# Differential attention: q's factor on the scores, roots and reciprocals over 192 columns, k rotated raw

## The reference, cut to what matters

```python
def rms_norm(x, g):
    x32 = x.astype(F32)
    y = x32 * lax.rsqrt(jnp.mean(x32 * x32, axis=-1, keepdims=True) + EPS)
    return (y * g.astype(F32)).astype(x.dtype)
...
def diff_softmax_pair(q, k, v, lam, scale):
    s = jnp.einsum('bqnd,bknd->bnqk', q, k).astype(F32) * scale
    p = jax.nn.softmax(s, axis=-1)
    ...
    w = p[:, :, 0] - lam * p[:, :, 1]
    return jnp.einsum('bhqk,bkhe->bqhe', w.astype(v.dtype), v)
...
    q = rms_norm(q.reshape(bsz, n, 2 * DIFF_HEADS, DIFF_DH), qn_g)
    k = rms_norm(k.reshape(bsz, n, 2 * DIFF_HEADS, DIFF_DH), kn_g)
    ...
    q_l = apply_axial_rope(q_l, cos, sin)      # x * cos + rot(x) * sin
    k_l = apply_axial_rope(k_l, cos, sin)
    ...
    o = rms_norm(o, subln_g) * (1.0 - lam_init)
    return (o.reshape(bsz, n, D_INNER) * jax.nn.silu(z)) @ w_out
```

## Time and profile before

| | us |
|---|---|
| median of three runs | 4011.03 (3999.76 to 4014.48) |
| the profiled execution | 4011.99 |
| its span, first to last instruction | 4010.3 |
| TensorE busy with matmuls | 3700.1, 92% |
| VectorE busy | 2045.9, 51% |
| ScalarE busy | 1197.8, 30% |
| the differential stage | from 1683 to 2852 |
| granted TensorE clock, mean of the span | 0.976 of full speed |

### The profile page before, as it was taken

How to read it: one execution, slowest core, us unless ns; L and a number is a source line. 1 busy time by engine, 2 the same in 40 slices (tenths; PEclk the granted TensorE clock), 3 DMA queues, 4 the chain that set the end, 5 groups by cost and what they waited for, 6 DMA issues and landing times.

```text
span 4010.3 us, 44586 instructions
## 1 busy us (share of the span) xinstructions
PE 3700.1 (92%) x16234; PEld 2354.2 (59%) x16234; DVE 2045.9 (51%) x3693; ACT 1197.8 (30%) x2200; POOL 143.2 (4%) x227
## 2 busy tenths in 40 slices
PE   5998999998889999899999999998798999999989
PEld 2445488873446888665656565564454555555554
DVE  3744353644545545455666666666214555555541
ACT  1213210112332101133434434343102454545530
POOL 6600000000000000000000000000000000000000
PEclk8998999999999999999999999999899999999999
DMA  7521334340013342410111011100011122212211
GB/s 149 143 75 48 95 95 106 89 112 24 21 53 105 95 116 74 116 37 27 32 31 31 26 31 31 31 26 26 23 51 58 53 58 58 58 53 57 58 32 53
DMA packets 456433, 246.27 MB, mean 61 GB/s; under 512 B 44256, under 2 KB 448352, under 8 KB 456320
## 3 DMA queue, kind: packets, MB, share of 16 engines
q1 hardware_dynamic: 420384, 216.15, 19.6%
q0 software_dynamic: 14144, 28.36, 2.7%
q10 hardware_dynamic: 21792, 0.22, 0.4%
HBM read 229.83 MB, written 14.80 MB: 61 GB/s over the span
## 4 chain that ended last, share of the span: by engine, by line
PE 79%; DVE 12%; ACT 4%; issue 2%; ACTq 1%; DMA 0%; DVEq 0%; SPq 0%
PE bank L466 19%; PE bank L1188 15%; PE bank L328 10%; PE bank L1709 8%; DVE rs L1934 4%; PE bank L1695 3%; PE bank L1036 3%; PE bank L1100 3%; PE bank L863 2%; PE bank L1731 2%; PE bank L1081 2%; PE bank L1742 2%; PE bank L846 1%; PE bank L1677 1%; PE bank L1345 1%
## 5 line engine op out<-in xcount | busy, mean ns | idle before, releaser
L1188 PE MATMUL bank<-hT,ring 128*128 128x512 f32 (+1 forms) x1664 | 634.1, 531 | 11.3 <-ACT hT L1599 6.0
L1709 PE MATMUL bank<-hT,ring 128*128 128x512 f32 x1504 | 509.0, 490 | 20.0 <-DVE big L1961 16.3
L1188 PEld LDWEIGHTS bank<-hT,ring 128*128 128x128 f32 x1664 | 311.1, 191 | 289.0 <-issue 276.2
L1709 PEld LDWEIGHTS bank<-hT,ring 128*128 128x128 f32 x1504 | 280.6, 190 | 244.4 <-issue 207.1
L328 PE MATMUL bank<-big,ring 128*128 128x512 f32 (+1 forms) x1024 | 389.2, 543 | 12.3 <-DVE big L1973 8.4
L328 PEld LDWEIGHTS bank<-big,ring 128*128 128x128 f32 x1024 | 195.8, 192 | 204.2 <-issue 183.9
L1088 ACT ACTIVATE arena<-bank 128x512 f32<-128x512 f32 (+2 forms) x224 | 118.4, 528 | 462.3 <-PE bank L1081 462.0
L466 PE MATMUL bank<-big,arena 128*128 128x256 f32 x1024 | 228.8, 379 | 0.0
L466 PEld LDWEIGHTS bank<-big,arena 128*128 128x128 f32 x1024 | 194.6, 190 | 26.5
L1056 DVE CUSTOM_DVE_ANT_0 arena<-bank,big 128x512 f32<-128x512 f32 (+2 forms) x152 | 101.3, 666 | 201.4 <-PE bank L1036 201.4
L1695 PEld LDWEIGHTS bank<-ring,hT 128*128 128x128 f32 x1536 | 179.2, 193 | 30.4 <-DVE arena L1928 17.1
(11 more groups left out here) (293 smaller groups left out, 5276.0 us busy)
## 6 DMA issues: line engine op xcount, KB each, us to landing
ring<-in_mlp_w SPq DMA_DIRECT2D x128, 512.0 KB, 5.5
ring<-in_a_w_in SPq DMA_DIRECT2D x64, 512.0 KB, 4.0
ring<-in_b_w_in SPq DMA_DIRECT2D x64, 512.0 KB, 4.0
ring<-in_mod_w SPq DMA_DIRECT2D x48, 512.0 KB, 4.0
ring<-in_even_w_in SPq DMA_DIRECT2D x32, 512.0 KB, 4.0
bias_d<-tb POOLq DMA_DIRECT2D x96, 128.0 KB, 3.3
big<-bias_d POOLq DMA_DIRECT2D x16, 768.0 KB, 5.4
ring<-in_a_w_out SPq DMA_DIRECT2D x16, 512.0 KB, 3.7
```

What stands on the lines that cost most here:

```text
L1188: mm = pe.matmul(bk(b + n)[0:m, 0:z - a], ring[s][:, k, 0:m], (rhs or hcol)(k, a, z), start=k == 0, stop=k == kt - 1)
L1709: mm = pe.matmul(flatb[2][:, a:z], ring[s][:, k, :], hT[:, k, a:z], start=k == 0, stop=k == KT - 1)
```

## The change

q's factor is no longer multiplied into q. The raw q (kept in the tile rs, called d_q) is rotated with a matrix that has the gain in it (rotq); its sum of squares is taken with the tokens on the partitions (six matmuls with two output columns), 12 columns per head in d_rq, and the factor is applied as the scale of the exponentials (exps) and in the negated maxima. k is rotated raw with its gain (rotk), and its factor multiplied in at the end (normed_k). For k and for the output the sum of squares goes to four groups of 32 partitions, 192 columns each, so that root and reciprocal run over 128 x 192 (d_rn, in the tile tb); a new matmul (broadcast, with the selecting matrices sel) spreads the factor over all partitions and 768 columns of bank 3, from which normed_k and y_normed read it. The places of the steps in each engine's order change with it.

```diff
+            dve.wait_ge(md_c, 8)
+            dve.tensor_scalar(rotq, rotx, cols[:, 5:6], None, ALU.mult).then_inc(md_c, 1)
+        def dve_rotk(dve):
+            dve.tensor_scalar(rotk, rotx, cols[:, 6:7], None, ALU.mult).then_inc(md_c, 1)
...
-        STEP = ["Tc'", "T0", "sq", "T1", "rq", "sk", "T2", "rk", "so'", "T3"]
+        STEP = ["Tc'", "T0", "rq", "sq", "T1", "rk", "sk", "T2", "bk", "so'", "bo'", "T3"]
...
 pe_dif:
                 if t == 0:
-                    pe.wait_ge(ds["m2"], h * 2 + 2)
+                    pe.wait_ge(ds["nr"], h + 1)
...
-                for a, z in spans(TT):
-                    mm = pe.matmul(flatb[3][:, a:z], lhs, d_sq[:, a:z], start=True, stop=True)
+                for j in range(4):
+                    mm = pe.matmul(flatb[3][32 * j:32 * j + 32, 0:G], lhs, d_sq[:, G * j:G * j + G],
+                                   start=True, stop=True, skip_group_check=True)
...
+            def stats_q():
+                pe.wait_ge(ds["sq"], st.sq["q"])
+                st.n_free(pe, "sq")
+                for t in range(6):
+                    mm = pe.matmul(flatb[3][:, 2 * t:2 * t + 2], d_sq[:, P * t:P * t + P], per_head,
+                                   start=True, stop=True, skip_group_check=True)
+            def broadcast(x, n):
+                pe.wait_ge(ds["rr"], n)
+                st.n_free(pe, x)
+                for i in range(2):
+                    for half_, r in enumerate((LO, HI)):
+                        mm = pe.matmul(bank[3][:, half_, G * i:G * i + G], sel[i][r, :], d_rn[r, :],
+                                       start=True, stop=True, skip_group_check=True)
...
             if make:
+                rotate_q()
                 project(1, "k", 0, 4)
-                stats("sq", st.sq["q"], b64)
+                stats_q()
...
             if make:
+                rotate_k()
                 project(2, "v", 0, 2)
-                rotate("rq", g * 2 + 1)
-                project(2, "v", 2, 4)
-                stats("sk", st.sq["k"], b64)
-                project(2, "v", 4, 6)
+                stats("sk", st.sq["k"], b64[:, 48:80])
+                project(2, "v", 2, 6)
...
             if make:
+                broadcast("bk", st.rr["k"])
                 project(3, "z", 0, 2)
-                rotate("rk", g * 2 + 2)
+            if old:
+                stats("so'", st.sq["o'"], ones[:, 0:32])
+            if make:
                 project(3, "z", 2, 4)
             if old:
-                stats("so'", st.sq["o'"], ones)
+                broadcast("bo'", st.rr["o'"])
...
 act_dif:
-                        mm = act.activation(d_p[s], flatb[s][:, 0:TT], ACT.Exp, bias=dst[:, 4 + s:5 + s],
-                                            accum_out=dst[:, 8 + s:9 + s])
+                        c = 2 * t + s
+                        mm = act.activation(d_p[s], flatb[s][:, 0:TT], ACT.Exp, scale=d_rq[e][:, c:c + 1],
+                                            bias=dst[:, 4 + s:5 + s], accum_out=dst[:, 8 + s:9 + s])
...
-                act.activation(rs[:, :], flatb[3][:, 0:TT], ACT.Sqrt, scale=1.0 / w, bias=eps).then_inc(ds["nf"], 1)
+                act.activation(d_rn, flatb[3][:, 0:G], ACT.Sqrt, scale=1.0 / w, bias=eps).then_inc(ds["nf"], 1)
...
 dve_dif:
+            def inverse(x, n):
+                st.n_done(dve, x)
+                dve.reciprocal(d_rn, d_rn).then_inc(ds["rr"], 1)
+            def normed_k():
+                dve.wait_ge(ds["bc"], st.rr["k"])
+                dve.wait_ge(ds["m2"], g * 2 + 2)
+                dve.tensor_tensor(spread(dk_(ge)), spread(d_nrm), bank[3][:, :, 0:2 * G], ALU.mult)\
+                    .then_inc(ds["nr"], 1)
...
             def y_normed(h, x, use):
-                st.n_done(dve, use)
-                dve.reciprocal(rs[:, :], rs[:, :]).then_inc(ds["rr"], 1)
-                dve.wait_ge(ds["rr"], st.sq[x])
+                dve.wait_ge(ds["bc"], st.rr[x])
...
             if on:
                 maxima(1)
+            if make:
+                rotated_q()
+            if on:
                 probs(1)
             if make:
-                normed("q", 0, 5)
-                evac(1, 1)
+                evac(1, d_raw)
+                inverse_q()
             if on:
                 maxima(2)
+            if make:
+                rotated_k()
+            if on:
                 probs(2)
             if make:
-                rotated(0, [(dq_(ge), ALL)])
-                normed("k", 1, 6)
+                inverse("sk", "k")
             if on:
                 maxima(3)
+            if make:
+                normed_k()
+            if on:
                 probs(3)
-            if make:
-                rotated(1, [(dk_(ge), ALL)])
             if old:
                 gated(h - 1, 1 - e, "o'", "pv'")
+                inverse("so'", "o'")
+                y_normed(h - 1, "o'", "so'")
             if on:
                 maxima(4)
                 probs(4)
-            if old:
-                y_normed(h - 1, "o'", "so'")
...
 before the stage, on TensorE and on VectorE:
+            pe.wait_ge(ds["ax"], 32)
+            pe.wait_ge(md_c, 12)
             run_dif(pe_dif, pe)
...
             dve_modulated(dve, 0, 0)
-            dve.wait_ge(ds["ax"], 16)
+            dve_rotk(dve)
+            dve.wait_ge(ds["ax"], 32)
             run_dif(dve_dif, dve)
```

More of the change, by code:

```diff
@@ L87, in constants @@
     c[:, C_AX + 512:C_AX + 1024] = np.tile(np.sin(ang), (2, 1))
+    for p in range(P):
+        if p % 16 == 0:
+            o = C_SEL + 128 * (p // 32 % 2) + 64 * (p // 16 % 2)
+            c[p, o:o + 64] = 1.0
     return c
@@ L1618, in program, with spread @@
         d_raw, d_nrm, d_sq = part(7680, TT), part(8448, TT), part(9216, TT)
+        d_q = rs[:, :]
+        G = TT // 4
+        tbf = tb[:, :, :].rearrange("p a b -> p (a b)")
+        d_rn = tbf[:, 0:G]
+        d_rq = [tbf[:, G + 12 * e:G + 12 * e + 12] for e in range(2)]
+        sel = [cst[:, C_CZ + P * i:C_CZ + P * i + P] for i in range(2)]
+        rotq, rotk = cst[:, C_RP:C_RP + P], cst[:, C_RM:C_RM + P]
+        per_head = b64.rearrange("p (s n) -> p s n", s=2)[:, :, 0]
+        def spread(x):
+            return x.rearrange("p (a n) -> p a n", a=2)
         axc = [part(9984, 512), part(10496, 512)]
@@ L1852, in act_dif @@
             if make:
-                act.wait_ge(ds["nr"], g * 2 + 1)
+                if old:
+                    act.wait_ge(ds["y"], h)
                 root(st.sq["k"], 64)
@@ new lines, in rotated_k @@
+            def rotated_k():
+                dve.wait_ge(ds["rot"], g * 2 + 2)
+                dve.tensor_tensor(d_t2, bank[3][:, 0, :], axc[1], ALU.mult).then_inc(ds["nf"], 1)
+                dve.tensor_scalar(d_nrm[:, S:TT], d_raw[:, S:TT], cols[:, 6:7], None, ALU.mult)
+                dve.scalar_tensor_tensor(out=d_nrm[:, 0:S], in0=d_raw[:, 0:S], scalar=cols[:, 6:7], in1=axc[0],
+                                         op0=ALU.mult, op1=ALU.mult).then_inc(ds["m1"], 1)
+                dve.wait_ge(ds["m1"], g * 2 + 2)
+                st.n_done(dve, "rk")
+                dve.tensor_tensor(d_nrm[:, 0:S], d_nrm[:, 0:S], d_t2, ALU.add).then_inc(ds["m2"], 1)
@@ L2011, in dve_dif @@
                 gated(h, e, "o", "pv")
+                inverse("so", "o")
                 y_normed(h, "o", "so")
```

106 lines of the change are left out of this document (61 added, 45 removed).

## The result

The changed kernel takes **4018.2 us** (median of 13 runs, 4015.05 to 4026.73) where the kernel before, on the same chip, takes 4011.1 (13 runs, 3998.69 to 4014.48). The ratio is **1.0029, 95% interval 1.0018 to 1.0039**: within 0.5% of no change, but clearly on the slower side, where 8 us less was forecast. The profiled execution took 4015.05 us, its span is 4013.3 us.

The account below looks back on a forecast made before the run. TensorE was taken to bound the differential stage. 14 steps of -0.47 (-6.6), first step -2.2, head +0.7 and tail +0.2 gave -7.9 us on 4011.99, 4004.1, so a median time of 4003.1 us; range 3986 to 4018.

Parts of the forecast that it names:

- the new wait between scores(3) and scores(4): In a loop step, TensorE waits 1.9 us at the output's broadcast for the 192-column reciprocal, where 1.79 went.
- The prediction's own sign of being wrong: Forecast wrong if two-column sum takes over 2 us, turn(3) waits for y_normed, or a step shortens over 1.5 us or grows.
- B: Rival: changing the array's shape costs more than 0.10 us a side; at double, 0.6 us a step, 4012 us; chance 0.14.
- C: Rival: a short matmul is priced by issue and load, not columns; +2.6 us a step, 4044 us; chance 0.08.
- Scores(1) to scores(2): Loop step stretch: q's rotation adds 0.87, the two-column sum takes 1.34 for the old 1.29; +0.92 us a step.
- A: Rival: exponentials' second operand hides (0.52 a step), two-column matmuls need one load (0.67); both 3984, one alone about 3994; chance 0.16.
- Scores(2) to scores(3): Loop step stretch: the 0.82 us wait before v goes, k's four-group sum takes 0.52 for 1.29; -1.59 us a step.
- Scores(3) to scores(4): Loop step stretch: broadcasts, output's sum, z and a 1.9 us wait give 12.45 against 12.6; -0.15 us (-0.4 to +0.5).
- Scores(4) to turn(4): Loop step stretch: four exponentials each pay 0.09 us for the scale operand, with nothing covering them; +0.35 us a step.
- First step and head: First step -2.2 us, having no old output to broadcast; head of stage +0.7, including +4.1 for q's projection awaiting rotk.
- Tail: Last head of the stage: -1.1 at probs(0), +4.2 at turn(3), -3.9 at the end, +1.0 for twelve exponentials; sum +0.2 us.
- Rival D: Rival: VectorE's share of the chain comes off, 48 reciprocals, 170 us; TensorE's waits allow only about 3970; chance 0.02.

Follow-up runs that it names:

- no_scale: The changed kernel without the exponentials' per-partition scale operand and with maxima negated without q's factor, so it computes something else; 4005.25 us, ratio 0.9986.
- after_again: The changed kernel as it is, with no edit, profiled once more; 4023.9 us.

## Why the prediction was wrong

**The step that failed** is the new wait between scores(3) and scores(4). Its size was right: 1.9 us forecast, 1.86 measured, the start of the broadcast 8.7 us after scores(3) where 8.6 was worked out. The price was wrong: I set 1.9 us against the 1.79 that went, and let a wait cost its length and no more. This one also costs 1.65 us of lower clock behind it in nine steps of 14, **+14.9 us** by the step lengths. Without them the stage would be 2.9 us shorter than before, not 12.0 longer. The prediction's own sign of being wrong, that a step grows, came with it: 70.66 on the mean against 69.77. No rival had it; B (4012), C (4044) and the range's top at 4018 were about other things, so a time of 4018.2 outside the range is not explained by any of them. The earlier trace rows show a wait of 1.79 us with full speed behind it; I took that for the rule for any wait of about this length, and did not ask how near it was to where it begins to cost more. The clock stood in the sum only at the head.

Point by point, with undisturbed steps where clock doesn't enter:

- **Scores(1) to scores(2)**, forecast +0.92: measured +0.84 (14.86 against 14.02). The two-column sum takes 1.26 us from its start to the next k product (2311.17 to 2312.43), 1.34 forecast. Rival C's 2.3 is excluded, and the part of A with one load for each.
- **Scores(2) to scores(3)**, forecast -1.59: measured -1.55. The wait before v is gone, the four-group sum takes 0.46 (2324.54 to 2325.00), 0.52 forecast.
- **Scores(3) to scores(4)**, forecast -0.15: measured +0.19 undisturbed, and the clock on top. The 0.34 are roundings of mine: the broadcast starts 0.1 later than I had it, and turn, scores and the quarter of z are some 0.2 longer together.
- **Scores(4) to turn(4)**, forecast +0.35: measured +0.35, with the wait of 0.43 that was to show it. no_scale confirms that it is the operand. The Trainium skill, ScalarE: Activation LUTs, What ACT_TABLE_LOAD costs, has some 93 ns for such an operand; the rows here agree with 986 - 897 = 89.
- **The step** therefore is 0.17 us shorter undisturbed, not 0.47: 14 x 0.3 = 4.2 us of the miss.
- **First step and head**, forecast -1.5 together: measured -3.15. The wait for the rotation matrix came (+4.49 for +4.1), v's wait shrank to 1.05 as said; q's projection itself got 0.7 us shorter (12.38 for 13.06), because more of it lies at the full clock when it starts later. I had let the slow start of the clock move with it.
- **Tail**, forecast +0.2: measured +2.7. The end gave -3.2 of the -3.9; the last step lost 5.8, not about 4: its granted clock went from 0.74 to 0.62, with TensorE waiting 7.57 us ahead of the broadcast. The four terms that the forecast names for turn(3) add up to 4.55, not to its +4.2.
- **Rival B**, a dearer change of the array's shape. The Trainium skill, TensorEngine Tiling (Array Packing), Key Properties, says that changing the tiling mode drains TensorE. Whether it does can't be told from these rows, only that it costs little: the two sums measured below what I gave them with 0.1 us a side, so B fell.
- **Rival D** fell as expected: 32 reciprocals are 3.6 us shorter each and q's 16, now over 12 columns, 4.7, some 190 us of VectorE, and an undisturbed step is 0.17 us shorter.

The change was good for more than its own order of work gives: with the wait taken away the loop is 27 us shorter and the clock's 15 come back, since with a reciprocal of 1.35 us the output's factor can be ready before turn 2. Whether the kernel before, with its reciprocals of 4.95 us, could be put in such an order was not tried.

**What stays open.** The length at which a wait begins to cost the clock is not one number: 1.70 us let it fall three times in no_scale, and 1.78 and 1.79 never in the two forms of the kernel before. The two kernels have different products around their waits, but which of these matter was not separated. Which steps fall goes by where the wait lies in the clock's raster (after_again); why the length that it takes differs between the two kernels is open.

## What to carry to other kernels

A wait on TensorE's path costs its length and no more only as long as the granted clock stays up behind it: when an edit makes a wait longer, or puts one in the place of another, read the granted clock and the length of every step, not one step, and price the wait at its length plus the time lost at the lower clock. Where such a wait can't be removed, a product without use in it can pay: it cost nothing here and gave back 11 us. Better is to ask, once an operation has become short, which of the work that stood behind it can now start a place earlier.

## What the runs showed of the hardware that I had not expected

- Between 1.79 us (0 of 14) and 2.10 us (11 of 14) in one and the same place of the kernel before, a wait of TensorE begins to cost its clock: 3.4 us at 0.50 behind it, 1.65 to 1.7 us of time. In the rest of such a step the clock stays at 1.00.
- Whether a wait of 1.86 us does it differs from step to step of the same loop, in the same way in two executions, and a shift of 3.8 us ahead of the loop changes the count from 9 to 11. What decides is where the wait begins on the raster of the clock's changes: 56 of 56 that begin less than 1.40 us behind one of its moments, 1 of 28 of the others.
- Useless work made the kernel faster: 14 products of 512 and 14 of 256 columns, 4018.2 to 4007.5 us.
- A reciprocal on VectorE costs by the column also at small sizes: 12 columns 0.22 us, 192 columns 1.345, 768 columns 4.95.
